# Feed-forward weights with their columns laid out by turns, and stationary operands read with a stride of two

## What is computed

```python
D_FF = 2816

def swiglu(x, w_in, w_out):
    a, b = jnp.split(x @ w_in, 2, axis=-1)
    return (jax.nn.silu(a) * b) @ w_out

x = x + 0.5 * swiglu(rmsnorm(x, ffn_norm[l]), w_ffn_in[l], w_ffn_out[l])
```

## Time and profile before

| | before |
|---|---|
| median of three runs | 2818.48 us |
| the profiled execution: its own time | 2817.12 us |
| its span, first to last instruction | 2815.3 us |
| mean granted TensorE clock | 0.996 |
| TensorE matmul busy | 2757.7 us (98%) |
| VectorE busy | 1844.8 us (66%) |
| ScalarE busy | 1299.2 us (46%) |
| bytes read from HBM | 464.99 MB, 167 GB/s over the span |

### The profile page before, as it was taken

One profiled execution on the slowest core, in us unless ns is written; L12 is line 12 of the kernel. 1 busy time (PEld: TensorE's weight loads), 2 busy tenths in 40 slices (PEclk: granted clock), 3 DMA queues, 4 the chain that ended last, 5 costly groups with the idle time before them and its releaser, 6 DMA issues.

```text
span 2815.3 us, 51162 instructions
## 1 busy us (share of the span) xinstructions
PE 2757.7 (98%) x22008; PEld 2642.5 (94%) x22008; DVE 1844.8 (66%) x3012; ACT 1299.2 (46%) x1860; POOL 71.7 (3%) x66
## 2 busy tenths in 40 slices
PE   8999999999999999999999999999999999999998
PEld 8999799999999979999999998899999999889998
DVE  5668676666665856666667647766666664676665
ACT  5445454443544545454444335544454433454443
POOL 0000000000000010000000001100000000110000
PEclk9999999999999999999999999999999999999999
DMA  7554356555554545555565573455555557444553
GB/s 261 177 174 131 116 172 197 180 188 186 183 181 150 150 135 160 181 185 173 184 215 174 189 171 120 106 180 184 180 173 187 178 180 171 135 106 161 187 184 102
DMA packets 481281, 474.60 MB, mean 169 GB/s; under 512 B 47104, under 2 KB 464416, under 8 KB 480928
## 3 DMA queue, kind: packets, MB, share of 16 engines
q1 hardware_dynamic: 477472, 460.83, 51.5%
q0 software_dynamic: 3584, 10.49, 1.4%
HBM read 464.99 MB, written 6.29 MB: 167 GB/s over the span
## 4 chain that ended last, share of the span: by engine, by line
PE 89%; DVE 6%; ACT 3%; DMA 1%; issue 1%; SPq 0%; DVEq 0%; ACTq 0%
PE ps L1056 34%; PE ps L949 31%; PE ps L1077 16%; PE ps L1118 2%; DVE WL L1888 1%; PE ps L1199 1%; PE ps L1163 1%; ACT WH L1509 1%; PE ps L996 1%; PE ps L1000 1%; PE ps L992 1%; DMA RAW<-in_w_in 1%; ACT REGION L1576 0%; PE ps L980 0%; DMA RAW<-in_w_branch 0%
## 5 line engine op out<-in xcount | busy, mean ns | idle before, releaser
L1888 DVE TENSOR_TENSOR WL<-RAW,WH 128x2048 fp32r<-128x2048 f32 (+2 forms) x390 | 871.3, 2240 | 425.0 <-ACT WH L1509 423.0
L1509 ACT ACTIVATE WH<-RAW 128x2048 fp32r<-128x2048 f32 (+2 forms) x398 | 736.9, 1864 | 163.6 <-DMA RAW<-in_w_in 91.3
L1077 PE MATMUL ps<-HL,WH 128*128 128x256 f32 x1408 | 394.0, 280 | 0.0
L1077 PE MATMUL ps<-HH,WH 128*128 128x256 f32 x1408 | 393.6, 280 | 0.0
L1077 PE MATMUL ps<-HH,WL 128*128 128x256 f32 x1408 | 393.1, 279 | 0.0
L949 PE MATMUL ps<-UH,WH 128*128 128x256 f32 x1328 | 382.5, 288 | 3.9 <-DVE WL L1888 3.9
L1056 PE MATMUL ps<-UH,WH 128*128 128x256 f32 x2688 | 374.8, 282 | 0.5 <-DVE WL L1888 0.5
L949 PE MATMUL ps<-UL,WH 128*128 128x256 f32 x1328 | 374.5, 282 | 0.0
L949 PE MATMUL ps<-UH,WL 128*128 128x256 f32 x1328 | 374.3, 282 | 0.0
L1056 PE MATMUL ps<-UL,WH 128*128 128x256 f32 x2688 | 373.5, 281 | 0.0
L1056 PE MATMUL ps<-UH,WL 128*128 128x256 f32 x2688 | 373.4, 281 | 0.0
(11 more groups left out here) (331 smaller groups left out, 3639.1 us busy)
## 6 DMA issues: line engine op xcount, KB each, us to landing
RAW<-in_w_ffn_in SPq DMA_DIRECT2D x88, 1024.0 KB, 5.1
RAW<-in_ffn_wi SPq DMA_DIRECT2D x88, 1024.0 KB, 5.1
RAW<-in_w_in SPq DMA_DIRECT2D x86, 1024.0 KB, 5.4
RAW<-in_w_ffn_out SPq DMA_DIRECT2D x32, 1024.0 KB, 4.7
RAW<-in_ffn_wo SPq DMA_DIRECT2D x32, 1024.0 KB, 4.7
RAW<-in_w_out SPq DMA_DIRECT2D x16, 1024.0 KB, 4.8
RAW<-in_w_ffn_out SPq DMA_DIRECT2D x16, 768.0 KB, 4.2
RAW<-in_ffn_wo SPq DMA_DIRECT2D x16, 768.0 KB, 4.2
```

The lines of the kernel that those rows point to most:

```text
L1077: last = nc.tensor.matmul(bank(n + side, 0, T), a[:, k, side * P:(side + 1) * P], b[:, k0 + k, :], start=k0 + k == 0 and a is wh and b is ...
L1509: nc.scalar.activation(split_ap(s, part_high(s)), raw_ap(s), ACT.Copy).then_inc(weights_high, 1)
L1888: v_.tensor_tensor(split_ap(s, part_low(s)), raw_ap(s), split_ap(s, part_high(s)).bitcast(FP), ALU.subtract)\
```

## The change

The host stores the feed-forward weights with each group of 256 columns in another order: what was column c of the first half goes to column 2c, and what was column c of the second half to column 2c + 1. The kernel then takes the even columns for side 0 and the odd ones for side 1, so that each output tile holds the same features in the same partitions as before. A stationary operand's read in SBUF now starts at byte 0 or 4 of the row of 256 columns and steps 8 bytes, over 1,024 bytes, where it was 512 contiguous bytes. The loads, their sizes, ScalarE's and VectorE's splits, the evictions, the waits and the order of the instructions on every engine are the same. `opening` gets a parameter, and its two uses in mixing parts keep contiguous operands (`beside`).

```diff
+            def beside(side):
+                return slice(side * P, (side + 1) * P)
+            def by_turns(side):
+                return slice(side, 2 * P, 2)
-            def opening(n, s, u):
+            def opening(n, s, u, half=beside):
...
-                        nc.tensor.matmul(bank(n + side, 0, T), wh[:, k, side * P:(side + 1) * P], UH[:, k, :], start=k == 0, stop=False)
+                        nc.tensor.matmul(bank(n + side, 0, T), wh[:, k, half(side)], UH[:, k, :], start=k == 0, stop=False)
...
-                        opening(p0, s, u)
+                        opening(p0, s, u, by_turns)
...
-                                last = nc.tensor.matmul(bank(n, 0, T), a[:, k, side * P:(side + 1) * P], b[:, k, :],
+                                last = nc.tensor.matmul(bank(n, 0, T), a[:, k, by_turns(side)], b[:, k, :],
...
-                                    last = nc.tensor.matmul(bank(n + side, 0, T), a[:, k, side * P:(side + 1) * P], b[:, k0 + k, :],
+                                    last = nc.tensor.matmul(bank(n + side, 0, T), a[:, k, by_turns(side)], b[:, k0 + k, :],
...
+_BY_TURNS = ["w_ffn1_in", "w_ffn1_out", "w_ffn2_in", "w_ffn2_out", "ffn1_wi_2", "ffn1_wo_2", "ffn2_wi_2", "ffn2_wo_2"]
...
+    for name in _BY_TURNS:
+        a = arrays[name]
+        arrays[name] = np.ascontiguousarray(a.reshape(a.shape[0], a.shape[1], -1, 2, P).swapaxes(-1, -2).reshape(a.shape))
```

More of the change, by code:

```diff
@@ L995, in opening @@
                     for k in range(DK):
-                        nc.tensor.matmul(bank(n + side, 0, T), wl[:, k, side * P:(side + 1) * P], UH[:, k, :], start=False, stop=False)
+                        nc.tensor.matmul(bank(n + side, 0, T), wl[:, k, half(side)], UH[:, k, :], start=False, stop=False)
                 for k in range(DK):
@@ L999, in opening @@
                     for side in range(2):
-                        last = nc.tensor.matmul(bank(n + side, 0, T), wh[:, k, side * P:(side + 1) * P], UL[:, k, :], start=False, stop=k == DK - 1)
+                        last = nc.tensor.matmul(bank(n + side, 0, T), wh[:, k, half(side)], UL[:, k, :], start=False, stop=k == DK - 1)
                         if k == DK - 1:
```

## The result

The changed kernel is slower: 2839.97 us in the median of four runs (2836.37 to 2841.85) against 2818.6 us, a ratio of 1.0075 with a 95% interval of 1.0057 to 1.0092. I had forecast 2737 us. The profiled execution took 2836.37 us, its span is 2834.6 us, 19.3 us above that of before.

The account below looks back on a forecast made before the run. TensorE's matmul pace was taken as the bound; at 111.5 ns, line 1056 saves 55.6 us, line 1077 26.6 and openings 3.3, less 4 lost at seams: -81.5 us, median 2737 us, range 2703 to 2885.

Parts of the forecast that it names:

- What bounds the kernel: Feed-forward stretches: time is the number of matmuls by their pace, 118.4 ns on line 1056, 117.8 on line 1077.
- the end at nothing: Strided weight loads in feed-forward matmuls: no price of their own, pace 111.5 ns, 85.5 us off before seam losses.
- a picture of the disturbance: Feed-forward matmuls: weight load and moving read both walk 1,024 bytes in step, colliding once at the start; pace 111.5 ns.
- No effect: Rival, feed-forward weight loads: paced by column count wherever columns lie; 2818 us, within 5 us; chance 0.14.
- Rival 3: Every feed-forward matmul: strided loads touch more lines, the disturbance doubles, 85.5 us more, 2904 us; chance 0.22.
- rivals 1 and 4: Feed-forward strided loads: 1, no effect, 2818 us, chance 0.14; 4, half rate, some 4,220 us, chance 0.04.

Follow-up runs that it names:

- e4: Kernel whose feed-forward parts each read operands their own way (stationary step 0, 1 or 2; moving operand of 256 or 128 columns, walking or standing), computing something else: 2797.57 us.
- e7: Kernel whose feed-forward parts each use another stationary step (0, 3, 4, 8, or contiguous one column off), moving operand standing or walking, computing something else: 3687.33 us.
- e3: Kernel before with only ffn1 parts strided and unused bytes putting base places at distances of 224, 256, 384 and overlay places at 96: 2822.83 us against 2819.85.
- e9: Kernel before, contiguous operands, with 224 unused bytes before RAW0 and 32 before REGION, overlay places as they were: 2784.53 us, ratio 0.9875.
- e5: Kernel before, contiguous operands, with tiles moved so every weight tile starts 64 bytes past a multiple of 256 from the activations: 2783.05 us, ratio 0.9867.
- e8: The kernel of e5 run once more, unchanged: 2788.19 us.

## Why the prediction was wrong

*What bounds the kernel* was right: the change acted through the pace of 12,672 matmuls, with no new wait.

This is a tally of paces measured afterwards, not a second forecast. Bounded from both sides, the price ran from nothing to 111 ns; I took the end at nothing, on a picture of the disturbance that spoke of the disturbance only.

*The rivals.* No effect, at 2818, was nearer than the forecast and still wrong. Rival 3 had the sign and the place, but not the mechanism: collisions fell, they didn't double, and its 2904 us were four times too much. What happened, a price of the stride itself of some 6 ns, lay between rivals 1 and 4, and I had no case there. The measured 2840 us lay inside the range of 2703 to 2885, which rival 3 had widened; the direction was wrong.

## What to carry to other kernels

When an operand's access pattern changes and no row has that pattern, its own price and its effect on others are two terms, and the first must be bounded by itself: two matmul streams that differ in it, with a moving operand that stands still, show it in one profile. Where a stream alternates loads of 128 columns with 256 moving columns, as this one does, the distance of the two in memory is worth trying before their stride: some 250 unused bytes gave 1.3% here. A step of four or eight elements in a stationary operand of the kind used here (4-byte elements) doubled the time of each matmul in the stream (233.3 and 237.7 ns against 111.7).

## What the runs showed of the hardware

- Weight loads of 128 fp32r columns set the pace of a matmul stream, with a moving operand that stands still, at 111.7 ns for steps of 0 and 1, 117.8 for 2, 173.3 for 3, 233.3 for 4, 237.7 for 8 (e4, e7); a start one column off costs nothing.
- With a walking moving operand the pace of contiguous operands depends on their distance, with a period of 256 bytes: 120 ns at 0 and 256 (before, e3), 116.7 or 117.8 at 224 (e9, before), 113.3 or 117.8 at 64 (e5).
- At 64 and at 192 bytes there are two stable paces for the same instructions and addresses, 113.3 and 117.8 ns (e5, e8, e9). They hold for hundreds of matmuls and can change after an interruption. That would spread the runs of such a kernel, and they are spread: 15 us over four runs of e5, against 6.6 over the nine of the kernel before beside them; only one of the four has a trace.
